# Filler redistributed over the mixer phase of a four-mixer decoder step, and another PSUM bank for one set of sample outputs

## What is computed

```python
z = x @ P['w_in']                          # 1024 -> 3592 columns, split among four mixers
hm = _mlstm(...)                           # A, gated matrix memory
ro = _retention(...)                       # B, retention with rotary positions
hg = _rglru(...)                           # C, a scan
y_w = _rwkv7(...)                          # D, delta rule
mix = jnp.concatenate([y_m, y_r, y_g, y_w], -1) @ P['w_out']
x = _layer_norm(ALPHA * x + mix, ...)
x = _layer_norm(ALPHA * x + _cross_attn(x, mem_k, mem_v, P['xa_wq'], P['xa_wo']), ...)
x = _layer_norm(ALPHA * x + jnp.square(jax.nn.relu(x @ P['w_up'])) @ P['w_down'], ...)
```

## Time and profile before

| quantity | value |
|---|---|
| median of three runs | 2240.8 us |
| the profiled execution | 2243.67 us, its span 2241.8 us |
| PE busy | 2188.2 us, 98% of the span |
| weight loads (PEld) busy | 1638.0 us |
| DVE, ACT, POOL busy | 1167.9, 427.9, 113.0 us |
| mean granted TensorE clock | 0.992 of full speed |

### The profile page before, as it was taken

How to read it: one execution, slowest core, us unless ns; L and a number is a source line. 1 busy time by engine, 2 the same in 40 slices (tenths; PEclk the granted TensorE clock), 3 DMA queues, 4 the chain that set the end, 5 groups by cost and what they waited for, 6 DMA issues and landing times. The chain is left out here.

```text
span 2241.8 us, 32592 instructions
## 1 busy us (share of the span) xinstructions
PE 2188.2 (98%) x13686; PEld 1638.0 (73%) x13686; DVE 1167.9 (52%) x1987; ACT 427.9 (19%) x899; POOL 113.0 (5%) x186
## 2 busy tenths in 40 slices
PE   7999999999999999999999999999999999999998
PEld 5877765547856888888988777655488478888888
DVE  5652236567466544675256422555765574448643
ACT  2332122021212221100023321221113022120000
POOL 0111101000000000000002111010001000000000
PEclk9999999899999999999999999998999999999999
DMA  7121124153542122222242111143335412223221
GB/s 275 64 76 40 32 66 124 55 176 131 189 169 94 48 103 76 75 76 75 76 134 76 38 41 59 43 124 111 115 150 208 158 67 76 76 76 106 82 75 41
DMA packets 136337, 217.30 MB, mean 97 GB/s; under 512 B 33672, under 2 KB 67776, under 8 KB 136064
## 3 DMA queue, kind: packets, MB, share of 16 engines
q1 hardware_dynamic: 133888, 211.02, 27.6%
q10 hardware_dynamic: 2304, 4.20, 0.5%
HBM read 198.39 MB, written 14.58 MB: 95 GB/s over the span
## 5 line engine op out<-in xcount | busy, mean ns | idle before, releaser
L738 PE MATMUL psum<-xT,ring 128*128 128x256 f32 (+1 forms) x768 | 203.5, 406 | 0.0
L2404 PE MATMUL psum<-tmp 128*128 128x272 f32 x768 | 181.2, 392 | 0.0
L2404 PEld LDWEIGHTS psum<-tmp 128*128 128x128 f32 x768 | 145.9, 190 | 30.1
L738 PEld LDWEIGHTS psum<-xT,ring 128*128 128x128 f32 x768 | 136.9, 189 | 34.4 <-issue 8.2
L735 PE MATMUL psum<-ring,ext 128*128 128x512 f32 x256 | 126.3, 629 | 1.6 <-ACT ext L1928 1.6
L688 PE MATMUL psum<-xT,ring 128*128 128x256 f32 (+1 forms) x512 | 120.4, 394 | 5.1 <-ACT big L1948 2.0
L2496 PE MATMUL psum<-big,ring 128*128 128x256 f32 (+2 forms) x768 | 119.9, 318 | 0.0
L2496 PEld LDWEIGHTS psum<-big,ring 128*128 128x128 f32 x768 | 112.4, 191 | 6.7
L688 PEld LDWEIGHTS psum<-xT,ring 128*128 128x128 f32 x512 | 96.3, 190 | 26.7 <-issue 5.0
L2404 PE MATMUL psum<-xT,ring 128*128 128x272 f32 x448 | 107.4, 393 | 0.0
L2404 PEld LDWEIGHTS psum<-xT,ring 128*128 128x128 f32 x448 | 85.0, 190 | 17.8 <-DMA ring<-in_w_up 0.3
(11 more groups left out here) (535 smaller groups left out, 3673.7 us busy)
## 6 DMA issues: line engine op xcount, KB each, us to landing
ring<-in_w_down SPq DMA_DIRECT2D x16, 2048.0 KB, 7.6
ring<-in_w_in SPq DMA_DIRECT2D x14, 2048.0 KB, 8.6
ring<-in_w_up SPq DMA_DIRECT2D x14, 2048.0 KB, 8.2
big<-in_cache_mem_k SPq DMA_DIRECT2D x16, 1024.0 KB, 7.7
ring<-in_xa_wk SPq DMA_DIRECT2D x4, 2048.0 KB, 9.0
ring<-in_xa_wv SPq DMA_DIRECT2D x4, 2048.0 KB, 11.7
ring<-in_w_out SPq DMA_DIRECT2D x4, 2048.0 KB, 8.7
ring<-in_xa_wq SPq DMA_DIRECT2D x4, 2048.0 KB, 10.5
```

The lines of the kernel that those rows point to most:

```text
L738: ins = pe.matmul(bank[:, :c.stop - c.start], wring[:, n % 2, k, i * P:(i + 1) * P], xTv[:, k, c], start=(k == 0), stop=(k == KC - 1))
L2404: ins = pe.matmul(ps[:, :HT], left[:, k, :], right[:, k, :], start=(k == 0), stop=(k == KH - 1))
```

## The change

No work is added or removed. The numbers that say how many filler units stand at a place are changed, and A's sample outputs go to bank 4 instead of bank 0. DVE's read of the normaliser state follows to bank 4.

```diff
-            FILL_OM, FILL_X, FILL_ST, FILL_SA = 3, 5, 3, 2
+            FILL_OM, FILL_X, FILL_ST, FILL_SA = 3, 4, 3, 1
...
-            FILL_AB = (6, ((6, 4), (10, 6), (10, 6), (10, 6)))
-            FILL_AB_S = 4
+            FILL_AB = (6, ((6, 4), (10, 6), (10, 6), (12, 12)))
+            FILL_AB_S = 6
...
-                        spare_products(pe, ("dpad", T), 3, (0, 1))
+                        spare_products(pe, ("dpad", T), 3 if T < 4 else 2, (0, 1))
...
-                                spare_products(pe, ("dsc", T), 5, (0, 1))
+                                spare_products(pe, ("dsc", T), 5 if T < 4 else 4, (0, 1))
...
-                            spare_products(pe, ("om", g, m), FILL_OM if m == 1 or g == 2 else 0, (0, 1))
+                            spare_products(pe, ("om", g, m), 2 if g == 2 or m == 2 else FILL_OM if m == 1 else 0, (0, 1))
...
-                            spare_products(pe, ("X", g, m), FILL_X, (0, 1))
+                            spare_products(pe, ("X", g, m), FILL_X if g < 2 else 2, (0, 1))
...
-                        spare_products(pe, ("inv", T), 3 if T < 4 else 1, (0, 1))
+                        spare_products(pe, ("inv", T), 2 if T < 4 else 1, (0, 1))
...
-                            spare_products(pe, ("UV", T), 1, (0, 1))
+                            spare_products(pe, ("UV", T), 2, (0, 1))
...
-                    outputs("A", 4, 0)
+                    outputs("A", 4, 4)
...
-                            sig.up(tt(ns, ns, psum[:, 0, 64:64 + 2 * NB].rearrange("p (q b) -> p q b", q=2), ALU.add), "oc2")
+                            sig.up(tt(ns, ns, psum[:, 4, 64:64 + 2 * NB].rearrange("p (q b) -> p q b", q=2), ALU.add), "oc2")
```

## The result

| | before | after |
|---|---|---|
| median, beside each other on one chip | 2241.19 us (6 runs, 2239.27 to 2250.24) | 2227.39 us (6 runs, 2226.85 to 2228.85) |
| the profiled execution, its span | 2243.67, 2241.8 us | 2227.42, 2225.6 us |
| mean granted clock in it | 0.992 | 0.998 |

The ratio is 0.9933 with a 95% interval of 0.9916 to 0.9950: 0.67% faster. Forecast were 2224 us and 2217 to 2235; the time lies in the range, 3.4 us above the forecast.

A forecast was written before the change was run, and what follows sets the result against it. The prediction took PE, busy 98% of the span, as the bound. From the profiled 2243.7 us it took 6.8 for waits and 10.1 for clock, giving 2226.8, then 2.9 to the median: 2224 us, range 2217 to 2235.

The forecast's parts named there:

- Fewer z products in the delta rule: Up to L1221, 21 z products fewer, 11.3 us of filler a layer moved later: taken as neutral, no gain or loss.
- Two z products between levels 1 and 2: At L1085, 1.08 us of filler covers PE's 0.89 us wait for DVE L1674, twice a layer: -1.8 us a layer.
- The filler at L1240: Eight z products (4.3 us) replace four kv products (3.70 us) under two waits that DVE ends: -0.9 us a layer.
- ACT's order: Behind L1240, ACT's late read-out and table load delay the squares that L688 needs: +0.5 us a layer.
- Bank 3: Kv halves begun inside a filler block wait for ACT at two places instead of one: +0.78 us a layer.
- Bank 4: A's sample outputs in bank 4 remove the 1.87 us wait at L1345; with L1365's 0.16 us, -2.0 us a layer.
- Waits together: Sum of all wait terms over PE's timeline: -3.4 us a layer, -6.8 us for both layers.
- The clock: Sample tile of A and B: low clock costs 12.9 us; one 6.5 us fall stays, costing 2.8; gain 10.1 us.
- a rival at 2221: Rival for the sample tile: without the L1345 wait the clock never falls, 12.9 us come back, 2221 us; chance 0.17.
- The last step: Whole kernel: from the profiled execution's 2226.8 us, 2.9 us taken off to reach the median, 2223.9 us.
- the delta rule loses its cover: Rival: PE reaches X, states and CV before ACT and DVE finish; up to 31.4 us lost, 2255 us; chance 0.05.
- The clock falls as before: Rival for the sample tile: 4-column runs themselves cause the falls, only waits are won, 2234 us; chance 0.14.

## Why the prediction was right

- *Fewer z products in the delta rule, 0.* Right: no wait at L1173 for L1699 or at L1099 for L2022. The margin at the states, put at 0.1 us, was as thin as read: one product of 0.54 us less costs 0.44 us of wait each time.
- *Two z products between levels 1 and 2, -1.8 a layer.* Right: the waits are gone in the changed kernel, and putting them back costs 3.3 us for two layers.
- *The filler at L1240, -0.9.* Mis-sized. I took 0.54 us a product from a tile of 288 columns and so 4.3 us for eight. The first eight took 3.83 us and the second eight 4.04, where the four kv products took 3.70. The first gained 0.13 us of cover and the three products ahead of them lost 0.26, so the first wait grew from 0.79 to 0.92 us; the second fell by the 0.34 us of the second eight, from 0.59 to 0.25. In layer 1 the two waits went from 1.38 to 1.17 us, so -0.2; in layer 2 the second is gone, but because the clock was low under it.
- *ACT's order, +0.5.* Right: 0.48 us, ACT L2068 as releaser, in both layers.
- *Bank 3, +0.78.* Right: 0.78 and 0.69 us, at the two places named, where one of 0.78 was.
- *Bank 4, -2.0.* The wait of 1.87 us and the 0.16 us went. But the edit had no part in it: with bank 0 the changed kernel is as fast. I had DVE's chain under six kv products in the sum and yet put the gain down to the bank.
- *Waits together, -6.8.* Measured -6.0.
- *The clock, -10.1: all four stretches but one short one.* Right that filler between the runs of L1345 brings the clock back, and close in size: 12.4 us, since the four stretches had cost 14.1 and not 12.9, and the one that is left costs 1.7 and not 2.8.

  That one fall was left is partly luck. I put it in the sample tile of A and B, where the profile has none; it came at L1240 of layer 2, and a clock of 0.50 in the delta rule was one of my own signs of being wrong. The prediction had that tile as its example of full clock. The place that I did name, the wait for bank 3 behind L1351, fell in another profile (without the two products between levels 1 and 2: 3.68 us for the four instructions that take 1.98). The piece I compared with, small runs between three or four dense products at full clock, was the right guide for the long falls, and the kernel with all filler ahead of the runs shows the reverse; short falls came in spite of it in three other profiles. The rule of the Trainium skill (TensorE: Matmul & The Clock Gate, section on HAM oscillation), by which I had a rival at 2221, does not explain this kernel: a fall came with PE busy 29.85 of 30 us. That none came behind the wait of 1.05 us does not count against it, since the page warns of long gaps.
- *The last step, 2.9 us off for the median.* This is the step that failed. The sum for the profiled execution was 2226.8 us and the profiled execution took 2227.42. I then took off the 2.9 us by which the profiled execution of before stood above its median. But those 2.9 us go with lower clock (0.992 on its mean, where most runs of 2239 to 2242 us have 0.994), and I had counted them already in the 12.9 that come back. Counted once, the forecast is 2226.8. That this is so near the 2227.4 measured is again partly luck, for three terms cancel: 0.8 us less from waits, 2.3 us more from the clock, and 1.9 us at the start of the program, which nothing in the profile of before could tell: 2226.8 + 0.8 - 2.3 + 1.9 = 2227.2.

Of the rivals, "the delta rule loses its cover" was near: the cover ends one product below the changed kernel. "The clock falls as before" was excluded by the profile of the changed kernel, and "not at all" by the fall in layer 2. What exactly starts a fall stays open: thin work was enough for a long one, but short ones came behind a wait and without one, among thin and among dense work.

## What to carry to other kernels

Dense filler that is taken from where the wait under it is already covered was worth most here between runs of very small matmuls, since it saved not only waits but the clock of what follows. Price both, from like instructions at either level, and take a disturbance off once: from the profiled execution or from the median. Once a kernel's end moves with the clock, a filled wait of 1 or 2 us can come back as a fall elsewhere, so look at the granted clock after each step, not only at the list of waits.

## What the runs showed of the hardware

- The granted clock fell to 0.50 with PE busy but for 0.15 us, when it worked on runs of 32 or 64 matmuls with 4 columns and 32-row products with little between them, and at that level it stayed for up to some 24 us of work without a longer pause (1540 to 1566 at 0.54 on the mean). With three or four 128x512 products between the runs it stayed at 1.00 but for stretches of 3.4 us, which came in three of the nine profiles of such kernels.
- The same program falls in one execution and not in another: 2227.1 to 2229.4 and 2238.2 to 2241.3 us with bank 4 alone. A median of few runs of such a kernel says little; the mean granted clock beside each run sorts them.
- The first 32 instructions of the input projection took 7.14 to 7.15 us in six profiles and 8.75 to 9.61 in seven, of kernels with the same start. The profile prints a clock of 1.00 for both, but its stored record of the clock begins at 18.2 to 19.7 us in the six, before these instructions start (19.4 to 20.1), and at 23.3 to 24.8 us in the seven. The extra time is half of what lies between their start and the first entry (at 24.1: 4.3 and 2.1 us; at 23.3: 3.3 and 1.6): until then PE ran at the lower level. Why the full clock comes later in some executions is not shown. The timed runs show a like step (2220.2 and 2222.4 us of one kernel, 2222.1 and 2224.1 of another).
- A half of a kv slab that is begun in the middle of a filler block waits 0.7 to 0.8 us for ACT's read-out of the one bank. With items of the list falling so that a half ends where a block ends, the wait is absent.
